# Attention projections of a fused transformer kernel on one Trainium2 core: 76 weight units multiplied in pairs by seven block products, and half of the norm ahead of them made in the stage before

## The reference

```python
def first_block(x, ...):
    for i in range(DEPTH):                       # 2 layers
        h = rms_norm(x, norm_pre[i])
        if i % 2 == 0: y = gmlp_mixer(h, ...)
        else:          y = dilated_attention_mixer(h, b_w_in, b_w_out, rel_bias)
        x = x + rms_norm(y, norm_post[i])
def dilated_attention_mixer(h, w_in, w_out, rel_table):
    z = h @ w_in                                 # 1024 x (9216 + 1024)
    qkv, gate = z[..., :B_QKV], z[..., B_QKV:]   # 3 groups x (q, k, v) x 16 heads x 64
    for gi, (window, dil) in enumerate(B_GROUPS):
        o, lse = dilated_window_group(q, k, v, table, dil, half_w)   # softmax(q k + bias) v
    wts = softmax(stack(lses), axis=0)           # the groups weighted by their log-sum-exp
    y = einsum(wts, outs) * silu(gate)
    return y @ w_out
```

## Time and profile before

| what | value |
|---|---|
| median of 3 runs | 3752.05 us (3745.39 to 3757.55) |
| the profiled execution's own time | 3743.86 us |
| its span, first to last instruction | 3742.3 us |
| mean granted clock of PE | 0.98 of full speed |
| PE busy / its weight loads busy | 3590.3 us (96%) / 2903.4 us (78%) |
| DVE / ACT / POOL busy | 53% / 35% / 3% |
| attention stage, first projection matmul to last output | 736.5 to 2134.4 us |

### The profile page before, as it was taken

The page is one execution under the profiler, slowest core; times in us unless marked ns, Lnnn a source line. Parts: engine busy times, 40 slices in busy tenths (PEclk is TensorE's granted clock), DMA queues, the critical chain, the costliest instruction groups (busy, mean ns, idle before and its releaser), DMA issues. The chain is left out here.

```text
span 3742.3 us, 48660 instructions
## 1 busy us (share of the span) xinstructions
PE 3590.3 (96%) x18034; PEld 2903.4 (78%) x18034; DVE 1977.6 (53%) x3847; ACT 1312.6 (35%) x2559; POOL 112.2 (3%) x137
## 2 busy tenths in 40 slices
PE   8999999899999999999998899999978999999999
PEld 6878887777777777777777687777976877888887
DVE  5387773353334445555555544544675667754443
ACT  4254443333323333333223434444323323232222
POOL 0000001000000000000000100000000000000000
PEclk9999999999999999999999999999989999999999
DMA  4222226411111112111111330111323322233333
GB/s 147 91 102 97 93 89 217 146 62 50 59 59 58 54 59 62 58 49 47 48 46 51 113 110 24 43 43 64 101 92 100 102 82 82 77 113 99 96 96 121
DMA packets 140884, 308.87 MB, mean 83 GB/s; under 512 B 31936, under 2 KB 70384, under 8 KB 140576
## 3 DMA queue, kind: packets, MB, share of 16 engines
q1 hardware_dynamic: 123904, 264.81, 22.0%
q0 software_dynamic: 14688, 33.22, 3.0%
q10 hardware_dynamic: 2112, 8.39, 0.6%
HBM read 256.55 MB, written 56.04 MB: 84 GB/s over the span
## 5 line engine op out<-in xcount | busy, mean ns | idle before, releaser
L142 DVE TENSOR_TENSOR all_w_lo<-all_w_raw,all_w_hi 128x1024 fp32r<-128x1024 f32 x295 | 361.1, 1224 | 337.8 <-ACT all_w_hi L137 337.7
L137 ACT ACTIVATE all_w_hi<-all_w_raw 128x1024 fp32r<-128x1024 f32 x295 | 310.1, 1052 | 478.9 <-PE om_z L155 261.2
L1465 PE MATMUL da_z<-all_hi,all_w_hi 128*128 128x512 f32 x736 | 305.7, 415 | 4.1 <-DVE all_w_lo L142 4.1
L1465 PE MATMUL da_z<-all_hi,all_w_lo 128*128 128x512 f32 x736 | 291.1, 396 | 0.0
L1465 PE MATMUL da_z<-all_lo,all_w_hi 128*128 128x512 f32 x736 | 289.8, 394 | 0.0
L1326 ACT ACTIVATE da_pt<-da_tr 128x512 f32<-128x512 f32 (+1 forms) x192 | 101.0, 526 | 485.7 <-PE da_tr L1518 485.7
L155 PE MATMUL om_z<-all_hi,all_w_hi 128*128 128x512 f32 x640 | 257.3, 402 | 7.9 <-DVE all_w_lo L142 4.7
L1334 ACT ACTIVATE at_p<-at_logit,da_pair_max 128x256 f32<-128x256 f32 (+1 forms) x384 | 178.0, 465 | 239.1 <-DVE da_pair_max L1720 238.7
L155 PE MATMUL om_z<-all_hi,all_w_lo 128*128 128x512 f32 x640 | 255.8, 400 | 0.0
L155 PE MATMUL om_z<-all_lo,all_w_hi 128*128 128x512 f32 x640 | 253.7, 396 | 0.0
L155 PE MATMUL pr_g<-all_hi,all_w_hi 128*128 128x344 f32 (+1 forms) x624 | 211.7, 339 | 10.7 <-issue 4.9
(11 more groups left out here) (692 smaller groups left out, 7781.0 us busy)
## 6 DMA issues: line engine op xcount, KB each, us to landing
all_w_raw<-in_w_mlp SPq DMA_DIRECT2D x128, 512.0 KB, 3.5
all_w_raw<-in_w_ug SPq DMA_DIRECT2D x48, 512.0 KB, 4.1
all_w_raw<-in_w_qkv SPq DMA_DIRECT2D x48, 512.0 KB, 3.7
all_w_raw<-in_w_in SPq DMA_DIRECT2D x27, 512.0 KB, 3.6
da_w_raw<-in_w_qkv SPq DMA_DIRECT2D x24, 512.0 KB, 3.6
all_w_raw<-in_w_bo SPq DMA_DIRECT2D x24, 512.0 KB, 3.5
all_w_raw<-in_w_v SPq DMA_DIRECT2D x20, 512.0 KB, 4.6
vhat<-ag_vst ACTq DMA_DIRECT2D x4, 2048.0 KB, 7.3
```

The costliest lines, as they stand in the source:

```text
L137: self.nc.scalar.activation(self.hi[b][:, :], self.raw[b][:, :], ACT.Copy).then_inc(self.hi_done[b], 1)
L142: self.nc.vector.tensor_tensor(self.lo[b][:, :], self.raw[b][:, :], self.hi[b][:, :].bitcast(F32), ALU.subtract).then_inc(self.lo_done[b], 1)
L1465: last = nc.tensor.matmul(z[h][:, :], wp[u][:, ws], ap[:, kk, cols], start=(kk == 0 and m == 0), stop=(kk == KT - 1 and m == 2))
```

## The change

1. The last four units of entry (q, k of pair 0, v of pairs 0 and 1) are still made by 48 matmuls each (`first_products`). The other 68 units of q, k and v and the 8 of the gate are taken in 38 pairs: (q, k) of one turn, (v, v) of two, two gates. Each pair is 7 block products (class `Seven`, like `Pairs`) of 12 matmuls, with 7 splits and 4 sums on DVE of 128x512 each, and 7 splits on ACT. Results leave PSUM by two copies on ACT (n2 from bx, n3 from bz), one exit on ACT (c11), and two sums and three exits on DVE (n2, n3, c22, c21, c12). The moving operands are `b11`, `b21`, `b22`, `t1` to `t4`, tiles of their own.
2. x is normed before it is split, so exits don't multiply by `inv`. q and k have two buffers each, so the copies of q_new and k_new go; v_new has two. Four banks (bx, by, bz, bv) go to the projection, and `tr` and `pv` keep one bank each: transposes of tile t wait for the copy of tile t-1, and the product with v for the scaling of tile t-1. The v transposes use `tr`, `pv` and `qk[0]`, so the first logits of a turn wait for DVE's copies of v.
3. A turn makes 21 half products of 6 matmuls (24 in the last turn), written out in `full`: none of the turns is a loop any more. 25 half products follow the last turn, with the 8 transposes back (`turn_y`) and the gating of y among them. In group 2 the merged result is stored to DRAM as in group 1 and read back.
4. In gmlp, under outputs 9 to 15, DVE and ACT make x + norm(y) of the first token half, its squares, their sum (one matmul at output 13), its norm, and the splits `b11` and `b21`. At the entry of the attention stage only the second half is left; its splits go to `b12` (cut out of `lo`) and `b22`, and t3, t2, t1 and t4 are made while PE runs the first four units.
5. The stage's loads come in quarters of a pair (256 KB).

The diff, cut to its core:

```diff
+                if n == KT + 5:
+                    pe.wait_ge(s_nacc, KT - 1)
+                    nc.tensor.matmul(cs[:, :], ones, nacc, start=True, stop=True).then_inc(s_ntot, 1)
...
+            def next_x(k):
+                if k == 0:
...
+                wait(dve, s_nx, k - 1)
+                nc.vector.tensor_tensor(nm[k % 2], x[:, k, first_half], inv[:, first_half], ALU.mult).then_inc(s_nm, 1)
+                dve.wait_ge(s_nm, k + 1)
+                dve.wait_ge(s_xin[k // 4], 64)
+                nc.vector.scalar_tensor_tensor(x[:, k, first_half], nm[k % 2], norms["post0"][:, k:k + 1], x_kept[:, k, first_half],
+                                               ALU.mult, ALU.add).then_inc(s_nx, 1)
...
+                if KT + 1 <= n < KT + 5:
+                    for k in range(2 * (n - KT - 1), 2 * (n - KT)):
+                        next_x(k)
+                        if k:
+                            next_total(k)
+                if n >= KT + 6:
+                    for k in range(4 * (n - KT - 6), 4 * (n - KT - 5)):
+                        next_norm(k)
+                    next_lo(n - KT - 6)
...
+class Seven:
...
+    ORDER = ("a11", "s3", "s1", "s2", "a22", "a12", "s4")
+    N = 7
...
+    def load(self, sp, j, part, unit):
+        before = self.N * (j - 1)
+        wait(sp, self.lo_done, before + {"a21": 2, "a11": 4, "a22": 5, "a12": 6}[part])
+        if part in ("a11", "a12"):
+            wait(sp, self.summed, 4 * j)
+        cols = slice(0, HALF) if part in ("a11", "a21") else slice(HALF, KT * P)
+        sp.dma_start(self.tile[part], unit[:, cols]).then_inc(self.loaded[part], 16)
+
+    def landed(self, eng, j, part):
+        eng.wait_ge(self.loaded[part], 16 * j + 16)
+
+    def plus(self, out, one, scale, two):
+        if scale == 1.0:
+            return self.nc.vector.tensor_tensor(out, one, two, ALU.add)
+        return self.nc.vector.scalar_tensor_tensor(out, one, scale, two, ALU.mult, ALU.add)
...
+    def add_four(self, dve, j):
+        t = self.tile
+        self.landed(dve, j, "a12")
+        dve.wait_ge(self.summed, 4 * j + 3)
+        dve.wait_ge(self.lo_done, self.N * j + 3)
+        self.plus(t["s4"], t["a12"], self.scales[j], t["s2"]).then_inc(self.summed, 1)
...
+    def split_hi(self, act, n):
+        j, i = divmod(n, self.N)
+        name = self.ORDER[i]
+        if name in self.loaded:
+            self.landed(act, j, name)
+        else:
+            act.wait_ge(self.summed, 4 * j + {"s1": 1, "s3": 2, "s2": 3, "s4": 4}[name])
+        wait(act, self.multiplied, n - self.slots + 1)
+        self.nc.scalar.activation(self.hi[n % self.slots], self.tile[name], ACT.Copy,
+                                  scale=self.scales[j] if name in ("a11", "a12") else 1.0).then_inc(self.hi_done, 1)
...
+    def split_lo(self, dve, n):
+        j, i = divmod(n, self.N)
+        name, b = self.ORDER[i], n % self.slots
...
+            last = self.nc.vector.tensor_tensor(self.lo[b], self.tile[name], self.hi[b].bitcast(F32), ALU.subtract)
+        last.then_inc(self.lo_done, 1)
...
+    def products(self, out, n, block, start, ks):
+        b = n % self.slots
+        for k in ks:
+            cols = slice(k * P, k * P + P)
+            for m, (wp, ap) in enumerate(((self.hi, block[0]), (self.lo, block[0]), (self.hi, block[1]))):
+                last = self.nc.tensor.matmul(out, wp[b][:, cols], ap[:, k, :], start=start and k == 0 and m == 0,
+                                             stop=k == KT // 2 - 1 and m == 2, skip_group_check=True)
+        return last
...
+        q, k_ = (q_even, q_odd), (k_even, k_odd)
...
+        bx, by, bz, bv = (st.ps(f"b{n}", [P, HALF]) for n in "xyzv")
...
+        pairs = []
+        for n in range(1, turns):
+            pairs += ([("v", n)] if n % 2 == 0 else []) + [("qk", n)]
+        pairs += [("gate", u) for u in range(0, KT, 2)]
...
+        PRODUCTS = (("b11", bx, True), ("t3", bz, True), ("t1", bv, True), ("t2", by, True), ("t4", bz, False), ("b21", bx, False), ("b22", bv, False))
...
+        full, short = (2, 2, 2, 2, 1, 2, 2, 1, 2, 2, 1, 2), (8, 2, 2, 1, 1, 1, 1, 1, 1, 1, 1, 1)
+        share_of = {n: short if n == 1 else (2,) * SUB if n == turns else full for n in range(1, turns + 1)}
...
-                with eng.Fori(2, B_PAIRS - 1) as hp:
-                    turn(base + hp, g, hp, g, hp - 1, g, hp - 2)
-                turn(base + B_PAIRS - 1, g, B_PAIRS - 1, g, B_PAIRS - 2, g, B_PAIRS - 3)
-            turn(turns, None, None, 2, B_PAIRS - 1, 2, B_PAIRS - 2)
...
-                for b in range(3):
-                    w.load(sp, b, n, a_in["w_qkv"][bass.ds(3 * n + b, 1), :, :].rearrange("a p n -> p (a n)"))
+            def block_loads(n):
+                j, r = divmod(n, Seven.N)
+                for at_, ahead, part_, i in ((5, 2, "a21", 1), (0, 1, "a11", 0), (1, 1, "a22", 1), (2, 1, "a12", 0)):
+                    if r == at_ and j + ahead < NP:
+                        seven.load(sp, j + ahead, part_, unit(j + ahead, i))
...
+            def block_work(n):
+                if n + 3 < NB:
+                    seven.split_hi(act, n + 3)
...
+                    return
+                if r == 0:
+                    wait(act, s_c12, j)
+                    act.wait_ge(seven.multiplied, n)
+                    nc.scalar.activation(n2, bx[:, :], ACT.Copy).then_inc(s_xc, 1)
+                if r == 1:
+                    wait(act, s_c22, j)
+                    act.wait_ge(seven.multiplied, n)
+                    nc.scalar.activation(n3, bz[:, :], ACT.Copy).then_inc(s_zc, 1)
+                if r == 5:
+                    free_to_leave(act, j, 0)
+                    act.wait_ge(seven.multiplied, n)
+                    out, view = dest(j, 0, 0)
+                    nc.scalar.activation(out, view(bx[:, :]), ACT.Copy).then_inc(s_c11, 1)
...
-            w.split(pe, 2, 0)
+            def first_products(u, h, ks):
+                b = u % 2
+                for k in ks:
...
+            for u in range(4):
+                w.split(pe, u % 2, u // 2)
+                if u == 3:
+                    first_products(u, 0, range(4))
+                    pe.wait_ge(s_acc, KT - 1)
+                    nc.tensor.matmul(pv[:, :], ones, acc_x[:, :], start=True, stop=True).then_inc(s_tot, 1)
+                    first_products(u, 0, range(4, KT))
+                else:
+                    first_products(u, 0, range(KT))
             for k in range(KT):
                 pe.wait_ge(s_lo, k + 1)
-                for u in (range(3) if k else (2,)):
...
+            def gemm(x):
+                n, half = divmod(x, 2)
+                j, i = divmod(n, Seven.N)
+                name, out, start = PRODUCTS[i]
+                if half == 0:
+                    pe.wait_ge(seven.lo_done, n + 1)
+                    if i < 4 and j == 0:
+                        pe.wait_ge(s_out, 4)
+                    for sem, count in (((s_c11, j),), ((s_c21, j),), ((s_c12, j),), ((s_n2, j),), ((s_zc, j + 1),), ((s_xc, j + 1),), ((s_c22, j + 1),))[i]:
+                        wait(pe, sem, count)
+                if j == 0 and name in made_lo:
+                    pe.wait_ge(s_blo, 2 * made_lo.index(name) + half + 1)
+                last = seven.products(out[:, :], n, blocks[name], start, range(2 * half, 2 * half + 2))
+                if half == 1:
+                    last.then_inc(seven.multiplied, 1)
...
+                    for x in work[n, s][0:1 if s == 0 else None]:
+                        gemm(x)
...
                         wait(pe, s_o, tiles * a)
+                        wait(pe, s_max, tiles * a)
...
-                            last = nc.tensor.transpose(dst[:, c0:c0 + P], v_new[:, off + m * P:off + m * P + P], ident)
+                            dst = (tr, pv, qk[0])[m // 4]
...
                         wait(pe, s_max, c)
                         k0 = t * P + (WINDOW if ag == 2 else 0)
...
-                        wait(pe, s_pt, c - 1)
+                        wait(pe, s_pt, c)
...
+            def block_work(n):
+                if n + 3 < NB:
+                    seven.split_lo(dve, n + 3)
+                j, r = divmod(n + 4, Seven.N)
+                if j < NP:
+                    if r == 1:
+                        seven.add_lower(dve, j)
+                        seven.add_left(dve, j)
+                    if r == 3:
+                        seven.add_three(dve, j)
+                    if r == 4:
+                        seven.add_four(dve, j)
+                j, r = divmod(n - 1, Seven.N)
+                if n < 1:
+                    return
+                second = 1.0 if pairs[j][0] != "v" else -1.0
+                if r == 3:
+                    dve.wait_ge(s_xc, j + 1)
+                    dve.wait_ge(seven.multiplied, n)
+                    nc.vector.tensor_tensor(n2, n2, by[:, :], ALU.subtract).then_inc(s_n2, 1)
+                    dve.wait_ge(s_zc, j + 1)
+                    dve.wait_ge(s_n2, j + 1)
```

(52 more changed lines are left out.)

965 lines of the change are left out of this document (568 added, 397 removed).

## The result

The changed kernel takes 3706.72 us (median of 4, 3692.44 to 3711.79) against 3750.29 for the kernel before on the same chip. The ratio is 0.9876, with a 95% interval of 0.9844 to 0.9908. The forecast was 3637, with a range of 3606 to 3690. The direction was right. The gain of 44 us is less than half of the 113 forecast, and the time lies outside the range.

The account below looks back on a forecast made before the run. Inside the turns PE, never idle, was taken as the bound: matmuls times their distance. Terms A to E, −122.4 − 9 − 9 + 22 + 4 = −114.4 us, gave a median of 3637 us, range 3606 to 3690.

Parts of the forecast that it names:

- A, fewer matmuls: Projection units on PE: 456 fewer matmuls at 0.2315 us, 105.6 us saved, all on the path.
- A, distance: Projection matmuls on operand tiles of their own: 0.2264 us apart rather than 0.2315, saving 16.8 us over 3288 matmuls.
- R3: Rival: layout doesn't set matmul distance, 0.2315 us stays, 16.8 us less gain, 3654 us; chance 0.05.
- B, entry: Attention stage entry: 12 us not worked rather than 20.7, −9 us, bounds 0 and −18.
- C, exit: Start of the attention stage's output: 3 us lost rather than 12.0, −9 us, bounds 0 and −12.
- D, DVE against PE: Turns: DVE's bundle at block product i = 4 stalls PE's logits, +22 us, bounds 0 and 85.
- E, clock: Entry of the attention stage: a stretch at the half clock behind the wait, +2 us.
- Costed at nothing: Next norm under MLP outputs, loads, queues of SP and POOL, ACT's extra work, y's transposes back: covered, 0 us.
- R2: Rival: DVE can't catch up, bundles set half their 4.5 us loose on PE per pair, 85 us, 3700; chance 0.14.
- R1: Rival: no stall in the turns, as DVE starts overlap more and PE has queued slack, 3615 us; chance 0.20.

Follow-up runs that it names:

- e5: Changed kernel with all of DVE's attention work in a sub-step ahead of its block work, except turn 1's s = 0: 3647.85 us, ratio 0.9721.
- e4: Changed kernel with rows of 520 values, 512 used, for four operand tiles each of the MLP and attention stages: 3707.39 us, one run.
- e3: Changed kernel with DVE's copies of v and the maximum ahead of block work, merge and scaling still behind it: 3680.58 us, ratio 0.9817.
- e7: e5 with the first copy of the values repeated 4, 6 or 8 times by group in turns 2 to 23: 3764.26 us, one run.
- e10: e5 with the first half's next norm moved from under MLP outputs 9 to 15 to behind output 15: 3677.47 us, ratio 0.9800.
- e9: e5 with n2, n3, c22 ahead of the lower split and sums in one pair in three (s = 4, odd turns): 3626.64 us, ratio 0.9666.
- e1: Changed kernel with DVE's copies of v ahead of block work in s = 0 alone: 3698.28 us, ratio 0.9871.
- e2: Changed kernel with DVE's bias and maximum ahead of block work in s > 0 alone: 3713.91 us, ratio 0.9900.
- e8: e5 with DVE making n2, n3 and c22 ahead of the lower split and two sums in each bundle: 3640.59 us, ratio 0.9710.

## Why the prediction was wrong, step by step

Up to the stage end the profiles differ by 44.0 us; the sum said 114.4.

- **A, fewer matmuls.** Right: 456 fewer. What they are worth shows in e5, where nothing covers it: a turn of 21 half products runs in 46.99 us with no wait, against 51.37. Of these 4.38 us, 18 fewer matmuls at 0.2315 make 4.17, the price used in the sum.
- **A, distance.** Right in cause (e4), wrong in size. In the changed kernel's turns the mean distance within a stream is 0.2300 us (2409 distances), and 0.2323 in the kernel before (2630). The 0.2264 of the earlier trace rows belongs to long streams. Taken by position behind a switch, the second to fourth distances are 0.231 to 0.234 here too, and only from the twelfth on do they stay at 0.2267; all but one of a turn's streams have 6 or 12 matmuls. So for the 3042 matmuls in the turns the gain is 3042 × 0.0023 = 7 us; the sum had 16.8. R3's doubt was half justified: layout sets the distance, but not at once.
- **B, entry.** The first matmul came at 735.40, and the wait ahead of the values' transposes was 2.47 us where I had put 2.7. Between the last sum and these transposes, 59.8 us hold 198 matmuls: 14 not worked rather than 12. About −7 instead of −9. PE's rows:

```profile
735.40 0.76 PE L1766 MATMUL da_bx<-na_b_hi,all_w_hi 128*128 128x512 f32 x1 [5.50 <-PEq L45]
758.64 1.12 PE L1776 MATMUL da_pv<-da_spare,all_ones 128*128 128x512 f32 x2 [1.64 <-DVE da_spare L1947]
763.45 0.50 PE L1766 MATMUL da_qk<-all_lo,all_w_hi 128*128 128x512 f32 x1 [0.90 <-DVE all_lo L1965]
```

- **C, exit.** The 5.82 us of the earlier trace rows are gone altogether; the outputs follow the last block product at once:

```profile
1988.03 0.39 PE L1214 MATMUL da_bv<-da_b_lo,all_w_hi 128*128 128x512 f32 x1
1988.26 0.40 PE L1901 MATMUL da_by<-all_hi,all_w_hi 128*128 128x512 f32 x1
...
2002.97 0.79 PE L1901 MATMUL da_bz<-all_hi,all_w_hi 128*128 128x512 f32 x1 [3.38 <-DVE all_w_lo L142]
```

  From the last product to the stage end it takes 114.5 us rather than 121.0: −6.5, not −9, as the wait for the second output unit's lower part grew from 2.78 to 3.38. (The text ahead of the prediction gives these outputs 48 matmuls each. They have 24 in either kernel, 384 in all; the 48 are the MLP stage's. No term of the sum used it.)
- **D, DVE against PE. This step failed.** The place was right to the sub-step: s = 0 in even turns, s = 4 in odd ones, and none of the waits inside the turns was for a load. The size was not: 52 us of waits in the 24 turns, where I had 22. The copies of the values took 22.0 where I had 8. The maximum took 24.0 where I had 14: 18.7 in the odd turns from 3 on, 3.1 in turn 1 and 2.2 in even turns, for which I had none. The scaling of o took 6.3 where I had nothing.

  In even turns PE's side held: it was ready for the even turn's first logits 6.7 us behind the turn's start (848.37 − 841.65), forecast 6.6 to 7.0. DVE's side was 8.0 in the sum, and 8.1 in the trace (849.72), but I had taken 0.2 to 0.6 off for starts that overlap. They overlap fully only where an instruction doesn't wait for the one just ahead: 845.45 to 846.06 is 0.61 us, but 846.06 to 846.84 and 846.84 to 847.64 are 0.78 and 0.80, n3 needing n2 and c22 needing n3, and 844.66 to 845.45 is 0.79, the second sum waiting for the first. And ACT's split ahead of the bundle began 1.74 us behind the turn's start, where I had 1.36. The hand-over to PE added 0.26. That makes 1.6 us rather than 0.4 to 0.9.

  In odd turns I gave ACT 0.63 for the split that starts the bundle. But ACT stood in its own queue first, as these rows of turn 3 show, whose block product began at 905.30:

```profile
906.07 0.50 ACT L1658 ACTIVATE at_p<-at_logit,da_pair_max 128x256 f32<-128x256 f32 x1
...
907.06 0.62 ACT L1196 ACTIVATE all_w_hi<-all_w_raw 128x512 fp32r<-128x512 f32 x1
...
912.72 0.51 ACT L1658 ACTIVATE at_p<-at_logit,da_pair_max 128x256 f32<-128x256 f32 x1 [3.93 <-DVE da_pair_max L2118]
```

  The split ran at 907.06 behind two exponentials, 1.8 us after the product began and not at once. So group 0's odd turns, "just hidden" by 0.3, waited 0.93 each; those of group 1 waited 1.22 to 1.79 and those of group 2 2.34, near the 1.7 and 2.2 of the forecast. The scaling of o, "counted already", was a stall of its own in group 2 (0.74 and 0.77 in an even turn) and in e3 the largest of all.
- **E, clock.** I had +2 behind the entry, and left out that each wait in a turn may bring the lower clock. That was 21 us in turns 2 to 23 (e5), and 3 more in turn 1 (busy PE 50.30 us at 0.94, in e5 47.32 at 1.00); e5 and e7 together show waits as its cause. The Trainium skill, "TensorE: Matmul & The Clock Gate", section "HAM oscillation — how this bites in real kernels", describes a kernel in which a recurring wait brings the clock down each time and the cost is paid over and over; the trace agrees in part: with waits of 0.9 to 3.6 us in each turn, 11 of the 22 turns stood at 0.92 to 0.97 and the other 11 at 1.00. The term belonged in D as a price on each wait, on average about half of the wait again.
- **Rest.** 30 (waits) + 22 (clock, 24 less the 2 of the sum) + 10 (distance) + 2.5 + 2 = some 66 of the 70 us are placed. The other 4 I did not take apart.
- **Costed at nothing.** Loads and queues of SP and POOL: right, no wait inside the turns names one. In the tail PE waited 1.2 us once for a load of y. The norm under the MLP's outputs: right within 1 us (e10).

R2 (3700) came nearest in number, and its reason was half wrong. Waits cost 52 us, not 85, and DVE could catch up (e5). As a number R1's 3615 is near what the design gives once DVE's order is mended, 3626.64 in e9; its reason, that the starts overlap enough, did not hold.

Behind the stage end the same 7632 matmuls took from 1594.0 us (e9) and 1595.5 (before) to 1603.8 (after) and 1612.0 (e5) at a granted clock of 0.97 (before), 0.96 (e9 and after) and 0.95 (e5). It isn't only chance of the execution that was profiled: all five runs of e9 (3620.54 to 3631.88) lie below all four of e5 (3640.43 to 3649.75), further than the 7.2 us of the attention stage, though on e9's chip the kernel before was 6 us slower (3753.0 against 3747.04). Why the code behind runs at another clock in one kernel than in another, no run here shows. So differences of medians hold some 10 to 20 us that the attention stage did not make, and what an edit did is better read from the stage end.

## What to carry to other kernels

An engine that is busy for 71% of the turns (DVE in the changed kernel, 751 of 1056 us) can still be what another waits for: when work is moved to it in bundles, write down what stands behind each bundle in its list, and put the steps that the bound engine waits for ahead of those that have several products of slack. Mend such an order for all the steps of the chain at once, since mending one hands the wait to the next (e1, e2, e3 against e5), and look at the in-order lists of the other engines too (e8). A wait of PE that recurs may bring the clock down: here all such waits together cost about one and a half times their length, though a single one may cost nothing more than itself.

## What the runs showed of the hardware

- The distance of fp32r matmuls of 512 columns is 0.2267 us where the rows of successive k join and 0.2314 where 8 values are left out between them (e4), and on joined rows it stays at the smaller value only from some 11 matmuls behind a switch on. Why it settles I can't say.
- Successive DVE instructions of 128x512 start 0.61 us apart, and 0.78 to 0.80 where one waits for a semaphore of the other; copies of 128x512 start 0.59 to 0.61 us apart without that wait (changed kernel) and 0.72 to 0.73 with it (e7). The Trainium skill, "VectorE: DVE Perf Modes", section "The DRAIN you can't avoid", holds that a semaphore between them costs nothing extra; these rows don't agree.
- A single wait of PE of 2.34 us a turn left the clock at 1.00 in some turns and lowered it to 0.97 in another (e7). One of 1.79 did both as well (changed kernel, turns 13 and 15).
